# Softmax sums of an encoder layer turned and spread by VectorE block transposes, and local attention in batches of two key steps and one

## What is computed

```python
h = x @ w_in                                    # q, k, v, z of mixers A and B, two merge gates
# mixer A: 8 query heads, 2 key heads, dim 64; each token sees the 128 tokens before and after it
s = q @ k.T * 64 ** -0.5 - slope * dist         # -inf outside the window
denom = sum(exp(s - m)) + exp(sink - m)         # a sink logit for each head joins the sum
ya = ((exp(s - m) / denom) @ v * silu(za)) @ w_proj_a
# mixer B: 8 query heads, 2 key heads, dim 64; RMSNorm and rotary on q and k; all 2048 keys
yb = (softmax(q @ k.T * 64 ** -0.5) @ v * silu(zb)) @ w_proj_b
y = (sigmoid(ga + b_a) * ya + sigmoid(gb + b_b) * yb) @ w_out
out = layer_norm(2 ** 0.25 * x + y) * ln_g + ln_b
```

## Time and profile before

| | |
|---|---|
| time, median of 3 runs | 682.38 us (682.15 to 682.48) |
| the profiled execution: its own time | 675.36 us |
| its span, slowest core (core 4) | 673.5 us (cores: 668.5 to 673.5 us) |
| TensorE's granted clock, mean over core 4 | 0.979 |
| TensorE matmuls | 610.6 us busy, 91%, 3832 instructions |
| VectorE | 318.2 us busy, 47%, 564 instructions |
| ScalarE | 407.9 us busy, 61%, 547 instructions |
| GpSimd | 125.5 us busy, 19% |

### The profile page before, as it was taken

One profiled execution on the slowest core, in us unless ns is written; L12 is line 12 of the kernel. 1 busy time (PEld: TensorE's weight loads), 2 busy tenths in 40 slices (PEclk: granted clock), 3 DMA queues, 4 the chain that ended last, 5 costly groups with the idle time before them and its releaser, 6 DMA issues.

```text
span 673.5 us, 12557 instructions; the slowest of 8 cores (668.5 to 673.5 us)
## 1 busy us (share of the span) xinstructions
PE 610.6 (91%) x3832; PEld 218.8 (32%) x3832; DVE 318.2 (47%) x564; ACT 407.9 (61%) x547; POOL 125.5 (19%) x193
## 2 busy tenths in 40 slices
PE   2889988998989599999999999999998999999990
PEld 0356532222223123333333333333332333344440
DVE  3198741124152323334664724265556325387457
ACT  0165578885876267676757577766775877731220
POOL 3268540013011011110121111011101110122022
PEclk9899999998999799999999999999999999999996
DMA  8988708066529445423566654445665534527403
GB/s 124 141 148 120 102 10 118 18 103 98 100 62 193 94 80 79 66 53 58 112 129 125 112 132 64 89 65 110 129 187 144 91 71 60 95 99 169 64 0 125
DMA packets 44816, 66.32 MB, mean 98 GB/s; under 512 B 16976, under 2 KB 19152, under 8 KB 44496
## 3 DMA queue, kind: packets, MB, share of 16 engines
q0 software_dynamic: 21520, 39.36, 39.1%
q1 hardware_dynamic: 23232, 26.17, 13.5%
HBM read 95.04 MB, written 8.52 MB: 154 GB/s over the span
## 4 chain that ended last, share of the span: by engine, by line
PE 72%; DMA 8%; DVE 7%; issue 6%; ACT 5%; SPq 1%; POOL 1%; DVEq 0%; ACTq 0%; POOLq 0%
PE PS L257 71%; DMA den<-D 4%; ACT PT L266 3%; DMA SZ<-ws 2%; DMA XT<-xT 1%; DMA R<-den 1%; SPq L276 1%; DVE QB L272 1%; ACT G L266 1%; DVE T L272 1%; DVE WR L269 1%; DVE PT L269 1%; DVE G L272 1%; DVE STT L574 1%; PE PS L405 1%
## 5 line engine op out<-in xcount | busy, mean ns | idle before, releaser
L266 ACT ACTIVATE PT<-PS 128x1024 bf16<-128x1024 f32 (+1 forms) x304 | 293.5, 1018 | 98.8 <-PE PS L257 98.0
L257 PE MATMUL PS<-XT,WROT 128*128 128x512 bf16 x896 | 221.3, 383 | 0.5 <-DVE G L272 0.2
L257 PEld LDWEIGHTS PS<-XT,WROT 128*128 128x128 bf16 x896 | 77.5, 98 | 127.2 <-issue 53.3
L276 POOL DMA_DIRECT2D WROT<-wg x100 | 53.6, 538 | 314.2 <-PE PS L257 313.0
L257 PE MATMUL PS<-PT,VX 128*64 128x512 bf16 (+3 forms) x688 | 99.5, 367 | 10.8 <-DVE PT L269 7.3
L272 DVE SCALAR_TENSOR_TENSOR G<-G,PS 128x512 f32<-128x512 f32 x64 | 43.5, 686 | 108.7 <-PE PS L257 83.0
L257 PE MATMUL PS<-QB,KB 64*128 64x512 bf16 x512 | 81.0, 383 | 6.2 <-ACT PT L266 5.8
L266 ACT ACTIVATE G<-PS,CVH 128x512 f32<-128x512 f32 x64 | 44.1, 689 | 58.3 <-PE PS L257 53.8
L257 PE MATMUL PS<-SZ,WR 128*128 128x512 bf16 x256 | 65.3, 386 | 10.4 <-DVE SZ L269 8.9
L257 PE MATMUL PS<-SZ,XT 128*128 128x384 bf16 (+1 forms) x256 | 57.4, 369 | 16.3 <-DMA XT<-xT 15.9
L257 PE MATMUL PS<-WR,T 128*128 128x512 bf16 x256 | 60.5, 380 | 0.2 <-DVE T L269 0.2
(11 more groups left out here) (67 smaller groups left out, 396.4 us busy)
## 6 DMA issues: line engine op xcount, KB each, us to landing
WROT<-wg POOLq DMA_DIRECT2D x100, 256.0 KB, 7.9
R<-den SPq DMA_DIRECT2D x64, 128.0 KB
T<-x SPq DMA_DIRECT2D x8, 512.0 KB
out<-T SPq DMA_DIRECT2D x8, 512.0 KB
QB<-x SPq DMA_DIRECT2D x6, 512.0 KB
out<-QB SPq DMA_DIRECT2D x6, 512.0 KB
SZ<-ws POOLq DMA_DIRECT2D x8, 256.0 KB, 9.1
XT<-xT POOLq DMA_DIRECT2D x2, 1024.0 KB, 11.4
```

The lines of the kernel that those rows point to most:

```text
L257: s.op("pe", lambda e: e.matmul(out, lhsT=lhsT, rhs=rhs, start=start, stop=stop, skip_group_check=skip), reads=reads, writes=writes)
L266: s.op("act", lambda e: e.activation(out=out, in_=in_, func=func, **kw), reads=reads, writes=writes)
L276: s.op(eng, lambda e: e.dma_start(out=out, in_=in_), reads=reads, writes=writes, dma=True)
```

## The change

The sums are kept in another layout, and no longer pass through DMAs.

- `ones` splits each step's queries in two halves of 256: quarter `2 * h + f` of `YBK` gets the sums of head `h` over all steps for query half `f`. There are four matmuls of 256 columns for a step in place of two of 512.
- `epilogue`: `turn` transposes the 32x32 blocks of `YBK` (128x256) into `TR` on VectorE, which puts the sum of each query into a column of its own block. One tick later `rec` adds the sink (A items), takes the reciprocal of the 8 columns that matter into `D`, copies four pieces of 32x8 so that both quarters of a head have both query halves, and a second block transpose that reads `D` by broadcast writes `R` (128x512). Two ticks later `final` multiplies. The copy on ScalarE, all five DMAs of an item, `den` in DRAM and `spread` are gone. `turn` is issued behind the `bias` of the next batch.
- `batches`: A items go as a batch of two steps and a batch of one.
- The fill's weights are 1.0 for batches of two steps, 0.9 for the batch of one, and 1.5 for the last batch of a B item if an A item follows.
- `slow` loads go at each tick that is free, `O`, `R` and `D` have two buffers in place of three.

```diff
-            elif slow and now[0] % 2 == 0:
+            elif slow:
                 slow.pop(0)()
...
             def ones(self):
-                lo, hi = self.lo, self.hi
                 for h in range(2):
-                    q = 2 * h + self.idx % 2
-                    mm(PS[32 * q:32 * q + 32, YBK, lo:hi], ONES[:], PT[:, self.slot, h, lo:hi], self.idx < 2, True,
-                       [("ONES",), ("PT", self.slot)], pk(YBK, h), skip=True)
+                    for f in range(2):
+                        a, b = max(self.lo, 256 * f), min(self.hi, 256 * f + 256)
+                        q = 2 * h + f
+                        if a < b:
+                            mm(PS[32 * q:32 * q + 32, YBK, a - 256 * f:b - 256 * f], ONES[:], PT[:, self.slot, h, a:b],
+                               self.idx == 0, True, [("ONES",), ("PT", self.slot)], pk(YBK, h), skip=True)
 
         def epilogue(kind, c, Q):
-            k = it_n[0] % 3
+            k = it_n[0] % 2
...
-            act(R[:, k, :], PS[:, YBK, :], AF.Copy, pk(YBK), [("R", k, 0), ("R", k, 1)])
-            for i_ in range(2):
-                dma("sp", D[:, k, i_, :], R[32 * i_:32 * i_ + 65:64, k, :].rearrange("h (p c) -> h p c", c=8),
-                    [("R", k, 0), ("R", k, 1)], [("D", k, i_)])
+
+            def turn():
+                s.op("dve", lambda e: e.transpose(out=TR[:, k, :], in_=PS[:, YBK, 0:256]), reads=pk(YBK), writes=[("TR", k)])
 
             def rec():
-                kd = [("D", k, 0), ("D", k, 1)]
-                d0, d1 = D[:, k, 0, :], D[:, k, 1, :]
-                stt(d0, d0, ESINK[:, c:c + 1] if kind == "A" else 0.0, d1, ALU.add, ALU.add, kd + [("ESINK",)], kd)
-                s.op("dve", lambda e: e.reciprocal(out=d0, in_=d0), reads=kd, writes=kd)
-                dma("sp", d_den[k].rearrange("(p c) -> p c", c=8), d0, kd, [("DEN", k)])
-
-            def spread():
-                for h in range(2):
-                    dma("sp", R[64 * h:64 * h + 64, k, :],
-                        d_den[k][512 * h:512 * h + 512].unsqueeze(0).to_broadcast([64, 512]), [("DEN", k)], [("R", k, h)])
+                d = TR[:, k, 0:256:32]
+                if kind == "A":
+                    s.op("dve", lambda e: e.tensor_scalar(out=d, in0=d, scalar1=ESINK[:, c:c + 1], scalar2=None, op0=ALU.add),
+                         reads=[("TR", k), ("ESINK",)], writes=[("TR", k)])
+                s.op("dve", lambda e: e.reciprocal(out=D[:, k, :, :], in_=d.unsqueeze(1).to_broadcast([128, 2, 8])),
+                     reads=[("TR", k)], writes=[("D", k, q, f) for q in range(4) for f in range(2)])
+                for q in range(4):
+                    o, f = q ^ 1, 1 - q % 2
+                    s.op("dve", (lambda q, f, o: lambda e: e.tensor_copy(
+                        out=D[32 * q:32 * q + 32, k, f, :], in_=D[32 * o:32 * o + 32, k, f, :]))(q, f, o),
+                        reads=[("D", k, o, f)], writes=[("D", k, q, f)])
+                s.op("dve", lambda e: e.transpose(
+                    out=R[:, k, :], in_=D[:, k, :, :].rearrange("p f c -> p (f c)").unsqueeze(2).to_broadcast([128, 16, 32])),
+                    reads=[("D", k, q, f) for q in range(4) for f in range(2)], writes=[("R", k)])
...
-            later(5, rec)
-            later(6, spread)
-            later(11, final)
+            later(1, rec)
+            later(2, final)
+            return turn
...
         def batches(steps):
             out, i = [], 0
             while i < len(steps):
-                if steps[i].kind == "B":
-                    out.append(steps[i:i + 2])
-                    i += 2
-                else:
-                    out.append(steps[i:i + 1])
-                    i += 1
+                n = 1 if steps[i].last else 2
+                out.append(steps[i:i + n])
+                i += n
             return out
...
-        def weight(bt):
-            return 1.0
...
+        def weight_of(i):
+            bt = all_b[i][1]
+            if len(bt) == 1:
+                return 0.9
+            return 1.5 if i + 1 < len(all_b) and all_b[i + 1][1][0].kind == "A" and bt[-1].last else 1.0
...
             if bt[-1].last:
-                epilogue(bt[-1].kind, bt[-1].c, bt[-1].Q)
+                turn = epilogue(bt[-1].kind, bt[-1].c, bt[-1].Q)
             for st in all_b[i + 1][1] if i + 1 < len(all_b) else ():
                 st.bias()
+            if bt[-1].last:
+                turn()
```

More of the change, by code:

```diff
@@ L186, in build_program @@
     d_ident = nc.dram_tensor("ident", [128, 128], F32, kind="ExternalInput").ap()
-    d_den = [nc.dram_tensor(f"den{i}", [1024], F32, kind="Internal").ap() for i in range(3)]
     d_out = nc.dram_tensor("out", [SEQ, DM], F32, kind="ExternalOutput").ap()
@@ L203, in build_program @@
         G = sb("G", [128, 5, 512], F32)
-        O = sb("O", [128, 3, 512], F32)
-        R = sb("R", [128, 3, 512], F32)
-        D = sb("D", [128, 3, 2, 8], F32)
+        O = sb("O", [128, 2, 512], F32)
+        R = sb("R", [128, 2, 512], F32)
+        TR = sb("TR", [128, 2, 256], F32)
+        D = sb("D", [128, 2, 2, 8], F32)
         QA = sb("QA", [128, 2, 4, 512], BF16)
@@ L829, in final @@
+                s.op("dve", lambda e: e.transpose(
+                    out=R[:, k, :], in_=D[:, k, :, :].rearrange("p f c -> p (f c)").unsqueeze(2).to_broadcast([128, 16, 32])),
+                    reads=[("D", k, q, f) for q in range(4) for f in range(2)], writes=[("R", k)])
             def final():
-                tt("dve", sz, O[:, k, :], R[:, k, :], ALU.mult, [("O", k), ("R", k, 0), ("R", k, 1), RG_SZ], [zk])
+                tt("dve", sz, O[:, k, :], R[:, k, :], ALU.mult, [("O", k), ("R", k), RG_SZ], [zk])
@@ L859, in build_program @@
         all_b = [(w, bt) for w, its in enumerate(windows) for bt in batches(make(its))]
-        def weight(bt):
-            return 1.0
-        left_b = [sum(weight(bt) for w, bt in all_b if w == k) for k in range(4)]
+        def weight_of(i):
[3 more added lines that the diff above has]
+            return 1.5 if i + 1 < len(all_b) and all_b[i + 1][1][0].kind == "A" and bt[-1].last else 1.0
+        weights = [weight_of(i) for i in range(len(all_b))]
+        left_b = [sum(x for x, (w, _) in zip(weights, all_b) if w == k) for k in range(4)]
         def start_batch(bt):
@@ L972, in build_program @@
             if bt[-1].last:
-                epilogue(bt[-1].kind, bt[-1].c, bt[-1].Q)
+                turn = epilogue(bt[-1].kind, bt[-1].c, bt[-1].Q)
             for st in all_b[i + 1][1] if i + 1 < len(all_b) else ():
                 st.bias()
+            if bt[-1].last:
+                turn()
             rem = sum(len(f[1]) for f in fill) + (len(cur[0][1]) - cur[0][4] if cur[0] is not None else 0)
-            share = rem * weight(bt) / left_b[w] + carry
+            share = rem * weights[i] / left_b[w] + carry
             n_mm = int(share)
@@ L980, in build_program @@
             pump(n_mm)
-            left_b[w] -= weight(bt)
+            left_b[w] -= weights[i]
             tick()
```

## The result

The changed kernel takes **696.57 us** (median of four), the kernel before 682.26 us in the same comparison. The ratio is 1.022 [1.018, 1.025]: the change makes the kernel slower, and the time lies outside the range that was given, 662 to 690 us. In some executions one die shows a lower clock and takes longer (here one of four, 727.61 us; the other three took 696.03 to 696.68 us): such executions count in the medians, which they move by less than 1 us save where it is said, but not in the ratios.

A forecast was written before the change was run, and what follows sets the result against it. TensorE was taken to bound windows 1 to 3. Terms -11.8 - 7.0 + 15.4 + 2.6 - 3.0 + 1.3 + 2.5 - 4.0 = -4.0 us gave 671.4 us profiled, 678.4 us timed; range 662 to 690 us.

The forecast's parts named there:

- VectorE, +2.5 us: Behind a B item's last batch, `rec` ahead of the third step's `bias`: 0.2 us for each of 12 items.
- Waits for exps, +15.4 and +2.6 us: A items: scores wait for the third step's exp, 1.28 us each in windows 1 to 3, half in window 0.
- The rival by which they cost nothing: A items' exp waits merely change places, so 18.0 us fall away: 660.4 us; chance 0.15.
- Waits for `PT` hidden, -3.0 us: Windows 1 to 3: most of 3.7 us of `PT` waits go, `bias` being issued well ahead of its `pv`.
- Start of window 1 and the end, -11.8 us: Waits for `SZ` and lower clock at window 1's start go, -10.7 us; window 3's last item's wait, 1.1 us.
- Window 0, -4.0 us: Window 0: 12 more fill matmuls where TensorE waited for exps, -2.5 us; eight copies off ScalarE, -1.5 us.
- Sums on TensorE, +1.3 us: `ones` of B items, 16 matmuls of 256 columns for 8 of 512: 0.02 us for each of 64 groups.
- The rounds do not pay for their loads, and that rival falls: Rival at `ones`: each added round costs its weight load's 0.1 us, 691.5 us; chance 0.07.
- A items, -7.0 us: Three changes of matmul kind less, 0.33 us, and shorter `ones`: 0.44 us for each of 16 A items.
- The 7 us carried over: Timed median before, 682.38 us, lay 7 us above the profiled 675.36 us; added to 671.4 us, giving 678.4 us.
- VectorE comes late: Fill groups want undrained banks behind B items' last batches and each `rec`: 16 in place of 2.5 us, 691.9 us; chance 0.13.
- three signs that would prove the forecast wrong: Exp waits much under 20 us; TensorE waiting for `G`, `T` or `O` over some 8 us; clock falling in window 0.

The follow-up runs named there:

- single steps: Changed kernel with A items again as three batches of one step and all fill weights 1.0; 687.43 us, 1.007.
- the quiet place: On top of single steps, where an A item follows, `rec` at the fourth tick and `final` at the fifth, behind its three `bias`; 666.59 us, 0.977.
- the one with copies on ScalarE: The fastest kernel with the four small copies of `D` in `rec` on ScalarE; 743.12 us (median of three), 1.090.
- the fastest kernel: Changed kernel with single steps and the quiet place together; 666.59 us, 0.977.
- scores one step ahead: Changed kernel with `start_batch` running ahead only when nothing is ahead; 688.78 us, 1.010; with `rec` at the third tick where an A item follows, 673.98 us.

## Why the prediction was wrong

- **VectorE, +2.5 us: the step that failed.** Its work was sized well (371.9 us against 370; the transposes 0.441 and 0.712 us against 0.42 and 0.69). What failed was "the cover is that fill banks are drained with a group's time to spare" and the 0.2 us an item. `rec` was put at "some 1.5 us"; it holds the engine for 1.8 us (B items) or 2.2 us (A items) in one piece, and the text named the place, ahead of the third `bias`, without following who stands behind it when a layer-norm instruction comes first. In windows 1 to 3 the chain cost 379.9 - 363.0 = 16.9 us on top of the batches, in place of 2.5: 9.2 us are waits (for `PT` 5.3, for `G` 3.9), half of the 17.1 us at the lower clock is the rest. In single steps it cost 14.6 us, and in the quiet place nothing.
- **Drains behind the batches, not in the sum.** The batches and weights alone bring `G` from 0.2 to 4.3 us and ScalarE's `G` from 1.5 to 3.2 us, 5.8 us in all, and single steps take them away again. The forecast named drains only beside VectorE's chain.
- **The clock, not in the sum.** In the changed kernel the long waits drew 20.5 us at 1.2 GHz that the kernel before does not have. The forecast priced such a stretch where a wait goes, at window 1, and not where waits come; it named it only as a sign to look for.
- **Waits for exps, +15.4 and +2.6 us: right.** 22.7 against 6.4 us, +16.3; twelve in windows 1 to 3, 12.9 us; in the kernel with the batches alone 22.4 us in 32 times. The rival by which they cost nothing falls: the batches alone cost 11.1 us in the stretch, with 11.6 us more of waits. But removing them from the changed kernel returned only half, since the chain on VectorE had been running under them.
- **Waits for `PT` hidden, -3.0 us: right for the batches, undone by the chain.** The batches alone take them from 7.3 to 0.4 us; in the changed kernel they are 8.8 us, in fewer and longer pieces.
- **Start of window 1 and the end, -11.8 us: right, a little high.** The wait for `SZ` and the lower clock behind it are gone (10.2 us at 1.2 GHz, of which the forecast counted the 5.94 us behind the second wait). The start of window 1 brings 8.4 us (+3.3 to -5.1) and the end of the kernel 1.8 us, together 10.2.
- **Window 0, -4.0 us: undone by the chain.** With the exps' 2.6 us, its A items and its sums the forecast for window 0 was -2.9 us; it is +3.3 us. With the batches alone it is -1.3 us, although TensorE waits for exps for 9.4 us in place of 6.4. In the changed kernel it waits for exps about as long (9.7 us), but 2.1 us more for `PT`, and 6.8 us lie at the lower clock, where the kernel before has 3.4 and the batches alone have none. That the copies leave ScalarE brought nothing that the end of the window shows.
- **Sums on TensorE, +1.3 us: right, too high.** A group of 16 takes 0.55 us, as the 8 did:

```profile
416.01 0.62 PE L257 MATMUL PS<-PT,ONES 128*32 128x256 bf16 x16
416.56 2.98 PE L257 MATMUL PS<-XT,WROT 128*128 128x512 bf16 x13
```

  The rounds do not pay for their loads, and that rival falls. The rule of the Trainium skill ("TensorE: Matmul & The Clock Gate", Part 3 on packing small matmuls), by which a load overlaps with matmuls in flight only where row groups differ, does not hold for this form: all four quarters use the same rows.
- **A items, -7.0 us: too high.** The groups of `ones` at A items did shrink from 0.54 to 0.44 us, 1.6 us in all. Of the rest, three changes of kind less at 0.33 us an item, little is seen: over 11 A items the batches alone cost 11.1 us with 11.6 us more of waits, so that the merging saved about 0.5 us in place of 3.6.
- **The 7 us carried over.** The changed kernel's median lies 0.5 us above its profiled execution. The kernel before has 7 us between them. The kernels here whose sums use no DMAs all have a median within 3 us of their profiled execution, save the one with copies on ScalarE (4 to 7 us); so the difference was no property to carry over. It hid a part of the miss: in the medians it is 696.57 - 678.4 = 18.2 us, in the traces 24.6. Why the kernel before scatters more was not found. The slowest core of its executions is nearly always one with the lowest granted clock (0.968 to 0.980), but the kernel with the batches alone has the same DMAs and scatters by only 0.7 us.

In the traces the forecast missed by 696.03 - 671.4 = 24.6 us. By place: for windows 1 to 3 behind their start it had 15.4 - 3.0 + 2.5 - 5.3 + 1.0 = +10.6 us, and 28.0 were measured, 17 us missed; in window 0 it missed 6 us, at the start of window 1 and the end 2 us. Of the 17 us about 13 belong to the chain, and the rest to the batches (drains, and the changes of kind that were not saved). The rival **VectorE comes late**, 691.9 us, with its place and its 0.5 us an item, 16 us in all, was the nearest to what happened; of its mechanism, waits for drains, it had a part, the other being `bias` and the clock. Of the three signs that would prove the forecast wrong, one came true: TensorE waits for drains more than 8 us. The second, a fall of the clock in window 0, is there (165.8 us, at a wait of 2.1 us for `PT`) and is 6.8 us long, but the kernel before has one of 3.4 us at nearly the same place.

What settles the cause is the comparison of single steps with and without the quiet place: the same sums on the same engine with the same instructions, 687.4 against 666.6 us. In windows 1 to 3 the fastest kernel runs level with the kernel before (-5.7 us after window 1's first A item, -6.3 us at the end of window 3), so its gain over the trace of before, 8.1 us, is the start of window 1 and the end. In the medians it is 2.3%, which includes the 7 us that the kernel before scatters above its trace. The change of the sums was good; its batches and the place of its chain made it slow.

## What to carry to other kernels

Price a chain that is moved onto an engine by its length in one piece and by what stands directly behind it in the queue, not by the engine's busy share: with VectorE at 54 to 56% in both, its place alone made 21 us. A place is quiet only against a given order: the same move that freed single steps set two chains behind each other in the batches of two and one. Where two delays run under each other, removing one shows half its price or less; try both together before judging either, and write the table of four. Measure the parts of a change alone as well: the batches alone, which were meant to help, cost 11 us in windows 1 to 3. Where a new wait of some 2 us on TensorE is forecast, count on half of a stretch at the lower clock of 3.4 to 6.8 us beside it, as one does when such a wait goes.

## What the runs showed of the hardware

Weight loads of 32 columns (96 ns mean) hide under rounds of four matmuls of 256 columns, one for each quarter of 32 columns: 16 of them take 0.55 us, as 8 of 512 do. A 32x32 block transpose on VectorE takes 0.441 us for 128x256 out of PSUM and 0.712 us for 128x512 read by broadcast; a copy of 32x8 takes 0.164 us there and 0.206 us on ScalarE, so four of them on VectorE cost nearly as much as one transpose of the full width. In the changed kernel's core 1, waits of TensorE of 1.95 to 3.45 us, and two of 1.0 and 0.9 us close together, each had 3.4 to 6.8 us at the lower clock at their end; single waits for exps of 1.1 to 1.4 us did not. It is no sure rule: with scores one step ahead, a wait of 2.17 us at 493 us and two of 1.95 us were not followed by any.

In the rows read here, no instruction of ScalarE or VectorE passed the one that stood waiting ahead of it: the ScalarE copies kept the exps behind them for up to 5.2 us of TensorE's time. "TensorE: Matmul & The Clock Gate" of the Trainium skill, on the array's architecture, says the same of these two engines (strict order, where only TensorE's queue reorders its loads), and these traces agree on the two.
